# Last projection by row tiles, row-tile waits of the branch projection, and the step-size weights in one block

## The reference

```python
h = _rmsnorm(x, norm_w) * (1.0 + scale[:, None]) + shift[:, None]
proj = h @ w_in
q, k, v, ga, u, gp, z, xbc, dt_raw, gl = jnp.split(proj, ...)
ya = _sink_window_attention(q, k, v, rel_bias, sinks) * jax.nn.silu(ga)
yb = _multiscale_pool(u, pool_w, pool_scale) * jax.nn.silu(gp)
yc = _ssd_branch(z, xbc, dt_raw, ...)      # dt = softplus(dt_raw + dt_bias), 16 columns
g = jax.nn.sigmoid(gl).reshape(b, s, 3, D_MODEL)
merged = g[:, :, 0] * (ya @ w_pa) + g[:, :, 1] * (yb @ w_pb) + g[:, :, 2] * (yc @ w_pc)
x = x + gate[:, None] * (merged @ w_out)
```

## Time and profile before

| | |
|---|---|
| median of 3 executions | 1201.2 us (1198.88 to 1203.27) |
| the profiled execution | 1203.91 us |
| its span, first to last instruction | 1202.2 us |
| TensorE busy, matmuls | 1152.5 us, 96% of the span |
| VectorE, ScalarE, GpSimd busy | 626.9, 513.4, 519.7 us |
| mean granted TensorE clock | 0.98 of full |

### The profile page before, as it was taken

One profiled execution on the slowest core, in us unless ns is written; L12 is line 12 of the kernel. 1 busy time (PEld: TensorE's weight loads), 2 busy tenths in 40 slices (PEclk: granted clock), 3 DMA queues, 4 the chain that ended last, 5 costly groups with the idle time before them and its releaser, 6 DMA issues.

```text
span 1202.2 us, 15182 instructions
## 1 busy us (share of the span) xinstructions
PE 1152.5 (96%) x5898; PEld 946.5 (79%) x5898; DVE 626.9 (52%) x757; ACT 513.4 (43%) x879; POOL 519.7 (43%) x381
## 2 busy tenths in 40 slices
PE   4899999999999999999979999999999999999997
PEld 4788888878888877887867888888788887778876
DVE  5806355668786444445340433565877754132364
ACT  4235257754435433223333534665445453232422
POOL 2335434434334455544415363434343425455541
PEclk9999999999999999999979999999999999999998
DMA  9654513334442445443313462322524423333322
GB/s 304 195 134 150 153 54 91 85 105 131 115 117 77 137 152 167 141 142 104 90 35 97 132 212 71 94 82 82 147 88 105 130 64 88 105 105 88 105 76 83
DMA packets 222200, 139.22 MB, mean 116 GB/s; under 512 B 11912, under 2 KB 212656, under 8 KB 222128
## 3 DMA queue, kind: packets, MB, share of 16 engines
q1 hardware_dynamic: 221480, 137.59, 40.0%
q10 hardware_dynamic: 648, 0.66, 0.2%
HBM read 135.08 MB, written 2.62 MB: 115 GB/s over the span
## 4 chain that ended last, share of the span: by engine, by line
PE 52%; DVE 3%; DMA 2%; ACT 1%; POOL 1%; issue 0%; SPq 0%; DVEq 0%; ACTq 0%
PE main L519 47%; DMA raw<-in_w_in 2%; PE psC L519 2%; DVE h_lo L1451 1%; PE psA L519 1%; PE psB L519 1%; POOL w_lo L481 1%; ACT w_hi L853 0%; DVE xbc L1406 0%; DVE y_lo L1446 0%; SPq L429 0%; PE psB L661 0%; ACT h_hi L853 0%; PE psB L681 0%; DVE misc L1286 0%
## 5 line engine op out<-in xcount | busy, mean ns | idle before, releaser
L481 POOL TENSOR_TENSOR w_lo<-raw,w_hi 128x512 fp32r<-128x512 f32 x352 | 504.2, 1454 | 650.1 <-ACT w_hi L853 650.1
L519 PE MATMUL main<-h_hi,w_hi 128*128 128x512 f32 x1152 | 463.2, 402 | 17.0 <-DVE h_lo L1171 6.3
L519 PE MATMUL main<-h_hi,w_lo 128*128 128x512 f32 x1152 | 452.9, 393 | 0.0
L519 PE MATMUL main<-h_lo,w_hi 128*128 128x512 f32 x1152 | 452.6, 393 | 0.0
L853 ACT ACTIVATE w_hi<-raw 128x512 fp32r<-128x512 f32 x352 | 203.8, 623 | 357.2 <-PE main L519 267.2
L519 PEld LDWEIGHTS main<-h_hi,w_hi 128*128 128x128 f32 x1152 | 218.8, 190 | 76.2 <-issue 22.3
L519 PEld LDWEIGHTS main<-h_hi,w_lo 128*128 128x128 f32 x1152 | 218.8, 190 | 47.1
L519 PEld LDWEIGHTS main<-h_lo,w_hi 128*128 128x128 f32 x1152 | 219.2, 190 | 45.4 <-issue 1.9
L1440 DVE TENSOR_TENSOR tmp<-main,misc 128x512 f32<-128x512 f32 x32 | 22.1, 690 | 178.1 <-PE main L519 172.2
L1286 DVE SCALAR_TENSOR_TENSOR misc<-main,cols,misc 128x511 f32<-128x511 f32 (+2 forms) x96 | 71.9, 749 | 65.6 <-ACT misc L853 63.0
L519 PE MATMUL main<-y_hi,w_hi 128*128 128x512 f32 x256 | 101.6, 397 | 2.6 <-DVE y_lo L1446 2.6
(11 more groups left out here) (226 smaller groups left out, 1083.6 us busy)
## 6 DMA issues: line engine op xcount, KB each, us to landing
raw<-in_w_in SPq DMA_DIRECT2D x128, 512.0 KB, 3.8
xbc<-in_w_ada SPq DMA_DIRECT2D x16, 512.0 KB, 4.8
zs<-in_w_ada SPq DMA_DIRECT2D x16, 512.0 KB, 4.6
raw<-in_w_pc SPq DMA_DIRECT2D x16, 512.0 KB, 3.8
raw<-in_w_out SPq DMA_DIRECT2D x16, 512.0 KB, 3.7
zs<-in_w_ada SPq DMA_DIRECT2D x16, 256.0 KB, 5.6
big<-in_w_ada SPq DMA_DIRECT2D x16, 256.0 KB, 6.1
tmp<-step_rows SPq DMA_DIRECT2D x8, 512.0 KB, 3.9
```

The lines of the kernel that those rows point to most:

```text
L481: nc.gpsimd.tensor_tensor(lo_b[:, cut, :], raw_b[:, cut, :], hi_b[:, cut, :].bitcast(F32), ALU.subtract).then_inc(s_split[b], 2 * BT_ // kt)
L519: return nc.tensor.matmul(o, a, b_, start=start, stop=stop)
```

## The change

In the last projection the first two tiles (couple 45, b = 0 and b = 1) are no longer computed one after the other. PE does row tiles 0 to 5 of b = 0, row tiles 0 to 5 of b = 1, then 6 and 7 of b = 0 and 6 and 7 of b = 1. Both take the waits for the split and for each row tile of the merged input. In the branch projection the b = 1 tile of couple 37 waits for each row tile k before its three matmuls, in place of one wait for all eight ahead of the tile; the tiles of couples 38 to 44 have no such wait. The step-size weights are laid out for each k as 48 columns: 16 high ones, 16 that are not written, 16 low ones. Two matmuls for each k (by `h_hi` and by `h_lo`) take the place of three; output rows 0 to 15 hold the high part's sum, rows 32 to 47 the low part's (now with the product low by low too), and VectorE adds the two in one more instruction, with a wait between the two.

```diff
-        dt_hi = y_hi[:, 0:1, 0:DTW].rearrange("p a n -> p (a n)")
-        dt_lo = y_lo[:, 0:1, 0:DTW].rearrange("p a n -> p (a n)")
+        dt_w = y_hi[:, 0:1, 0:DTW].rearrange("p a (k n) -> p (a k) n", n=3 * SH)
...
-                nc.gpsimd.tensor_copy(dt_hi[:, 0:KT * SH], dtraw).then_inc(s_dth, 1)
+                dt_raw = dtraw.rearrange("p (k n) -> p k n", n=SH)
+                nc.gpsimd.tensor_copy(dt_w[:, :, 0:SH], dt_raw).then_inc(s_dth, 1)
                 pool.wait_ge(s_dth, l + 1)
-                nc.gpsimd.tensor_tensor(dt_lo[:, 0:KT * SH], dtraw, dt_hi[:, 0:KT * SH].bitcast(F32),
+                nc.gpsimd.tensor_tensor(dt_w[:, :, 2 * SH:3 * SH], dt_raw, dt_w[:, :, 0:SH].bitcast(F32),
                                         ALU.subtract).then_inc(s_dts, 1)
...
+            def tile_part(l, u, b, k0, k1, ready):
+                if k0 == 0:
+                    pe.wait_ge(s_evac[b], l * COUPLES + u)
+                for k in range(k0, k1):
+                    pe.wait_ge(s_split[b], part_count(l, u, k // BT_))
+                    pe.wait_ge(ready, l * KT + k + 1)
+                    mm(main[b][:, :], w_hi[:, b, k, :], h_hi[:, k, :], k == 0, False)
+                    mm(main[b][:, :], w_hi[:, b, k, :], h_lo[:, k, :], False, False)
+                    last = mm(main[b][:, :], w_lo[:, b, k, :], h_hi[:, k, :], False, k == KT - 1)
+                if k1 == KT:
+                    last.then_inc(s_tile[b], 1)
...
                 for k in range(KT):
-                    cut = slice(k * SH, k * SH + P)
-                    mm(psC0, dt_hi[:, cut], h_hi[:, k, :], k == 0, False)
-                    mm(psC0, dt_hi[:, cut], h_lo[:, k, :], False, False)
-                    last = mm(psC0, dt_lo[:, cut], h_hi[:, k, :], False, k == KT - 1)
+                    mm(psC0[0:3 * SH, :], dt_w[:, k, :], h_hi[:, k, :], k == 0, False)
+                    last = mm(psC0[0:3 * SH, :], dt_w[:, k, :], h_lo[:, k, :], False, k == KT - 1)
...
                 for u in range(U_C, U_OUT):
                     h_tile(l, u, 0)
-                    pe.wait_ge(s_yc, (l + 1) * KT)
-                    tile(l, u, 1, y_hi, y_lo)
-                h_tile(l, U_OUT, 0, s_m)
-                h_tile(l, U_OUT, 1)
+                    tile(l, u, 1, y_hi, y_lo, ready=s_yc if u == U_C else None)
+                for k0, k1 in ((0, KT - 2), (KT - 2, KT)):
+                    for b in range(2):
+                        tile_part(l, U_OUT, b, k0, k1, s_m)
...
-                ts_(v, psC0[0:SH, :], hpar[:, 0, l:l + 1], None, ALU.add).then_inc(s_dtx, 1)
+                ch.link(ts_(v, psC0[0:SH, :], hpar[:, 0, l:l + 1], None, ALU.add))
+                tt(v, v, psC0[2 * SH:3 * SH, :], ALU.add).then_inc(s_dtx, 1)
```

More of the change, by code:

```diff
@@ L71 @@
 BANDW = 192
-DTW = (KT - 1) * SH + P
+DTW = KT * 3 * SH
 def rel_buckets():
```

## The result

The kernel after takes 1194.9 us (median of 13 executions, 1191.53 to 1198.36) against 1203.27 us for the kernel before on the same chip (13 executions, 1198.72 to 1208.43). The ratio is 0.9933, 95% interval 0.9919 to 0.9946: a gain of 8.1 us (6.5 to 9.7), where 13.6 us were forecast. The direction was right, the size was not, and the 1194.9 us lie above the range. Of the distance to the forecast of 1187.6 us, 2.1 us are the starting point: the forecast counted from 1201.2 us, the median of three executions, and thirteen give 1203.27.

A forecast was written before the change was run, and what follows sets the result against it. PE was taken as the bound, with matmuls under way in 96% of the span. Step sizes 3.7, branch tile 3.2 and last projection 6.7 us sum to 13.6 us: 1201.2 to 1187.6 us, range 1184 to 1193.

The forecast's parts named there:

- The step-size block: Step-size group: 8 matmuls fewer in each layer at 0.2308 us, 1.85 us a layer, 3.69 us for two.
- The rival that their weights stand in the way: Step-size group: half-column weights not loaded behind the stream, gain nil, 1191.3 to 1191.7 us; chance 10%.
- the price of two switches of shape: Step-size group: switching from full array to half the columns and back, 0.4 us at most in two layers, counted as 0.
- Its slip: VectorE's step-size chain slips 0.77 us against PE, covered by 0.90 us slack at tile (6, 1); cost 0, bound 0.5 us.
- a sign of being wrong: Listed under "Wrong": among others, a wait of PE for weights at tile (6, 1) near 113 us.
- The branch tile: First branch tile: with waits per row tile its gaps go, 2.07 + 0.87 us and 0.28 us of restarts, 3.2 us.
- The last projection: Last projection's first two tiles: 8.9 us of lost time recovered, less 2.2 us for a new gap, 6.7 us.
- The b = 1 tile is now wanted early: Last projection, couple 45: GpSimd's split halves end near 558.1 and at 559.72, so both in time.
- 1.6 us of slow matmuls: Last projection, layer 0: part of the 4.47 us lost, matmuls at 1.2 GHz behind the gap for three microseconds.
- Couple 46: Last projection: its weights' split starts only 6 matmuls ahead; new gap 0.95 us, with restart 1.1 us a layer, 2.2 us.
- only half arrives: Whole kernel: something other than PE sets later stages, some 1194.5 us; 13% together with both costs at once.
- The rival in which the clock falls again behind the new gap: Last projection, before couple 46: 1.6 us in each layer stay lost, 1190.8 us; chance 12%.

The follow-up runs named there:

- the last kernel: Whole change plus earlier last merge, b = 0 ended 12 matmuls sooner, and gate-slab sum started with a multiplication: 0.9875 to the kernel before, median 1188.65 us.
- the steps and the branch alone: Two runs, each one part put into the kernel before: step-size edit 0.9974 (3.1 us), first branch tile's row-tile waits 0.9973 (3.2 us).
- the new order: Whole change plus earlier last merge, with b = 0 of the last projection ended 12 matmuls sooner: 0.9896 to the kernel before, 12.5 us.
- the mended last projection alone: Kernel before with only the last projection's reorder, plus the earlier last merge and b = 0 ended sooner: 0.9965, 4.2 us.
- the last projection alone: Kernel before with only the change's new order of the last projection's first two tiles: 0.9991 (1.1 us), again 0.9993.
- the fillers: Kernel before with 2 and 6 dummy matmuls ahead of the last projection's waits for row tiles 6 and 7: 0.9986, 1.7 us.

## Why the prediction was right in part, point by point

**The step-size block: right.** 16 matmuls in 3.70 us in both layers, 0.231 us each, the value taken from the earlier trace rows. Before, the group took 5.55 us from its first start to the next one behind it (82.87 to 88.42 in layer 0), so the gain is 1.85 us in each. The rival that their weights stand in the way is out. So is the price of two switches of shape: 16 x 0.2268 = 3.63, so both together cost at most 0.07 us in a layer. The rule cited from the Trainium skill, "TensorEngine Tiling (Array Packing)", Key Properties, by which each switch drains the engine, would have made that 0.32; the trace doesn't bear it out, and whether 48 columns are another mode to the engine no row shows.

**Its slip: the bound held, the mechanism only in part.** The forecast was 0 with a bound of 0.5 us. Over the 240 matmuls behind the group PE loses 0.12 us in layer 0 and 0.35 in layer 1 (0.23 of it the gap), in all 0.5. That there is a wait at tile (6, 1) was named as a sign of being wrong. The extra instruction takes 0.77 us with its wait, as forecast; but VectorE's multiplication L1249 takes 1.04 us where it took 1.33, so the slabs start only 0.31 us later against PE. Then the two slab instructions take 0.95 us more, and the raw load goes out 1.25 us later against PE (20.0 us behind the group's end for 18.8), more than the 0.90 us of slack in layer 0. The load itself then took 0.34 us less than before in layer 0 and 0.20 us more in layer 1, whose slack was 1.24 us: 1.25 - 0.34 = 0.91 and 1.25 + 0.20 = 1.45 us, just over the one and 0.21 over the other. The sum had set the slack against the extra instruction alone. In the trace of the last kernel the gap is gone in both layers.

**The branch tile: right.** Forecast 3.2 us; by the trace 2.20 us in layer 0 (9.23 to 7.03 us for the 31 starts from the last gate matmul on) and 1.03 in layer 1, by timing alone 3.2 us. No later wait took its place.

**The last projection: wrong.** Forecast 6.7 us, measured 1.1 and 0.8. Two steps failed.

The first is "The b = 1 tile is now wanted early, its first half at 555.56 + 18 x 0.2268 = 559.64 and its second at 562.4 ... both in time." Besides its input a tile waits for two things, the split and the bank. I checked the split for b = 1, and bank 0, and not bank 1. That bank still held the last branch product. The price is 1.28 us + 0.14 us in each layer, 2.8 us in all; the kernel that frees the bank earlier has no such gap and gains 2.1 us more than the change.

The second is the term "1.6 us of slow matmuls", counted as lost by the gap and so as won without it, 3.2 us in two layers. The stretch is real in the first trace, but it doesn't belong to that gap alone. In the ten layers traced with the old gap open it stood there in six, so on average this place loses 0.6 x 1.6 us in each layer, 1.9 us in all, and not 3.2. And it can come elsewhere. In layer 0, the four traces in which both the branch tile's gap and the old gap are open have one stretch each, twice behind the one and twice behind the other. Where the branch tile's gap is open and the last projection's is closed or filled, it stands behind the branch tile's in four of five. A list of the matmuls of more than 0.55 us in each trace, over both layers, without the start and the change of layers, gives 24, 24 and 16 for the kernel before and 15 each for the steps and the branch alone, mean 19; for the other nine traces 7 to 16, mean 13. Each costs about 0.2 us, so (18.8 - 12.8) x 0.2 = 1.2 us; at the change of layers the latter have on average 2.4 more, which takes 0.5 us back.

The timings agree with little or nothing of it on average. Without any gain from the clock, the last projection is worth 8.9 - 3.2 - 2.1 (couple 46) - 2.8 (bank 1) = 0.8 us, 0.7 by the table; measured 1.1 and 0.8. The whole change is 3.7 - 0.5 + 3.2 + 0.7 = 7.1 us, measured 8.1 (6.5 to 9.7); with the bank freed 10.0, measured 10.2; with the new order 11.7, measured 12.5; the mended last projection alone 5.3, measured 4.2 (2.8 to 5.5). The upper ends for the last projection alone (2.4 us from 0.9980, 2.5 from 0.9979) leave at most some 1.8 us for the clock; 3.2 is excluded. Two kernels lie above their sums with the whole interval: the fillers (1.7 us, 0.1 to 3.2, where the sum is 0) and the last kernel (15.1 us, 13.2 to 16.9, where it is 12.1).

Every timed execution has its mean granted clock on record, and that tells most of what is left. With two levels, 1.00 and 0.50, the time at half rate is 2 x (1 - clock) x span; most of it lies at the start and the change of layers, in every kernel. For 73 executions of the kernel before, on three chips, it is 44.3 us on average (mean clock 0.9816). For the 85 of the nine kernels without the old gaps, or with them filled, it is 44.5 us (0.9814). Among executions of one kernel (182, each compared with its own kernel's mean), 1 us more at half rate goes with 0.35 us more time. So over these kernels the closed gap brings nothing from the clock on average; my estimate from the scatter is 0 with 0.7 us to either side. Single kernels do differ, each against the kernel before on its chip: the fillers have 3.8 us less at half rate, which is worth 1.3 us, the last kernel 4.6 us less, 1.6 us, and the mended last projection alone 4.0 us more, which costs 1.4 us. With that the sums are 1.3, 13.7 and 3.9 us, measured 1.7, 15.1 and 4.2. Why one order of work has more half-rate time elsewhere than another stays open.

**Couple 46: right.** Forecast 0.95 us and a restart, idle 0.8 by the profile; it is 566.49 - 565.29 - 0.23 = 0.97 us, idle 0.82. The restart is 0.08 us and not 0.14: the next start comes 0.31 us later, not 0.34.

**The rivals.** The measured time is near that of "only half arrives" (1194.5 us), but not by its mechanism: nothing but PE sets the stages in question, and each gap closed came through to the end. The rival in which the clock falls again behind the new gap would have given 1190.8 us. Its stretch isn't in the trace, but its price has to be paid all the same, since in the old kernel it was only partly there to be won. That rival and the missed bank together are 1187.6 + 3.2 + 2.8 = 1193.6 us; counted from the 1203.27 us of thirteen executions it is 1195.7, near the 1194.9 measured.

## What to carry to other kernels

When work is moved forward, list every semaphore that the moved instruction waits for, its inputs and its output bank too, and for each ask what its owner does at the new time; the wait that was satisfied for free in the old order is the one that is missed. A stretch of half-rate matmuls in one trace isn't the price of the gap ahead of it: look at a second execution of the same kernel before it is put into a sum. When an order creates a new gap, try where the piece can be cut so that both buffers have time: here it was enough to end b = 0 behind two row tiles of b = 1 and not behind six.

## What was not expected of the hardware

The granted clock behind a gap isn't a property of the gap: in one execution 1.75 us idle were followed by 1.00, and 1.74 us idle, at the same place of the other layer, by 0.56. Over ten such layers the clock fell in six. The mean clock of the span was 0.980 to 0.983 in all executions profiled here, with the gaps, without them, and with dummy matmuls in them.

A group of 16 matmuls with 48 columns of stationary operand and 512 of moving ran at 0.231 us each between groups of the full array. Their weights hide behind the stream as those of 128 columns do, though both share all rows. A load of 48 columns takes 0.12 us, one of 128 takes 0.19, and each starts while the matmul ahead is under way. Timeline of the weight loads in layer 0 of the kernel after:

```profile
83.83 0.19 PEld L519 LDWEIGHTS main<-h_hi,w_lo 128*128 128x128 f32 x1
84.06 0.12 PEld L519 LDWEIGHTS psC<-h_hi,y_hi 128*48 128x48 f32 x1
84.28 0.12 PEld L519 LDWEIGHTS psC<-h_lo,y_hi 128*48 128x48 f32 x1
```

The Trainium skill, "TensorE: Matmul & The Clock Gate", Part 3, The mechanism, lets a weight load overlap a running matmul only where the row group differs; the 0.231 us show no such limit here. The same section also lets a load into the background weight buffer be pulled ahead of running matmuls, and the 0.231 us would fit that; which buffer a load goes to, no row shows.
